# Memory's cross attention from one float32 product to three products of rounded parts

## The reference, cut to what matters

```
def memory_cross_attention(q, mem_n, w_mem_kv):
    mk, mv = jnp.split(mem_n @ w_mem_kv, 2, axis=-1)
    qh = q.reshape(B, S, XATTN_HEADS, HEAD_DIM_2)
    kh = mk.reshape(B, M, XATTN_HEADS, HEAD_DIM_2)
    vh = mv.reshape(B, M, XATTN_HEADS, HEAD_DIM_2)
    lg = jnp.einsum('bshd,bmhd->bhsm', qh, kh).astype(jnp.float32) * (HEAD_DIM_2 ** -0.5)
    p = jax.nn.softmax(lg, axis=-1).astype(q.dtype)
    return jnp.einsum('bhsm,bmhd->bshd', p, vh).reshape(B, S, C_WIDTH)
...
        out_c = memory_cross_attention(qc, mem_n, w_mem_kv[layer]) * jax.nn.silu(gc)
        y = (jax.nn.sigmoid(ma) * (out_a @ w_branch_a[layer])
             + jax.nn.sigmoid(mb) * (out_b @ w_branch_b[layer])
             + jax.nn.sigmoid(mc) * (out_c @ w_branch_c[layer]))
```

## Time and profile before

| | us |
|---|---|
| median of 3 runs | 913.99 |
| lowest and highest | 913.52, 914.01 |
| the profiled execution's own time | 914.61 |
| its span in the trace | 912.4 |
| TensorE busy in the span | 904.5 (99%) |
| VectorE busy | 610.7 (67%) |
| ScalarE busy | 507.8 (56%) |

### The profile page before, as it was taken

One profiled execution on the slowest core, in us unless ns is written; L12 is line 12 of the kernel. 1 busy time (PEld: TensorE's weight loads), 2 busy tenths in 40 slices (PEclk: granted clock), 3 DMA queues, 4 the chain that ended last, 5 costly groups with the idle time before them and its releaser, 6 DMA issues.

```text
span 912.4 us, 12831 instructions
## 1 busy us (share of the span) xinstructions
PE 904.5 (99%) x4764; PEld 764.8 (84%) x4764; DVE 610.7 (67%) x1007; ACT 507.8 (56%) x820; POOL 40.4 (4%) x53
## 2 busy tenths in 40 slices
PE   9999999999999999999999999999999999999997
PEld 7888788888888898878888888887888888888886
DVE  4897697766663756769766666386656577574665
ACT  5786655555562456665555555255557664655444
POOL 0100000440000001000000000001000000000000
PEclk9999999999999999999999999999999999999999
DMA  9844526777573577552855556354664465555651
GB/s 322 294 164 139 185 93 231 233 228 249 192 238 112 108 225 231 159 187 93 293 183 190 198 190 241 122 171 149 198 201 131 159 202 166 167 157 186 198 169 72
DMA packets 72604, 169.32 MB, mean 186 GB/s; under 512 B 11288, under 2 KB 32944, under 8 KB 71904
## 3 DMA queue, kind: packets, MB, share of 16 engines
q1 hardware_dynamic: 70080, 157.73, 53.3%
q0 software_dynamic: 2320, 10.58, 3.5%
q10 hardware_dynamic: 144, 0.20, 0.1%
HBM read 167.43 MB, written 1.06 MB: 185 GB/s over the span
## 4 chain that ended last, share of the span: by engine, by line
PE 95%; DVE 2%; DMA 1%; ACT 1%; SPq 0%; issue 0%; DVEq 0%; ACTq 0%
PE psum L851 20%; PE psum L1037 14%; PE psum L732 8%; PE psum L737 8%; PE psum L734 8%; PE psum L1040 8%; PE psum L1069 7%; PE psum L1073 4%; PE psum L962 3%; PE psum L972 3%; PE psum L966 3%; PE psum L1173 2%; PE psum L709 1%; PE psum L1208 1%; PE psum L1189 1%; DMA stage<-in_w_ab_in 1%
## 5 line engine op out<-in xcount | busy, mean ns | idle before, releaser
L1792 DVE TENSOR_TENSOR base_lo<-stage,base_hi 128x1024 fp32r<-128x1024 f32 (+3 forms) x221 | 261.1, 1206 | 103.9 <-ACT base_hi L1373 102.7
L1373 ACT CAST base_hi<-stage 128x1024 fp32r<-128x1024 f32 (+3 forms) x221 | 222.5, 1035 | 57.2 <-PE psum L737 22.5
L1792 DVE TENSOR_TENSOR extra_lo<-stage,extra_hi 128x1024 fp32r<-128x1024 f32 (+1 forms) x68 | 80.7, 1212 | 45.6 <-ACT extra_hi L1373 45.4
L732 PE MATMUL psum<-base_hi,xt 128*128 128x512 f32 (+2 forms) x256 | 100.7, 393 | 0.0
L737 PE MATMUL psum<-base_hi,xt 128*128 128x512 f32 (+2 forms) x256 | 98.4, 384 | 0.0
L734 PE MATMUL psum<-base_lo,xt 128*128 128x512 f32 (+2 forms) x256 | 98.2, 384 | 0.0
L1373 ACT CAST extra_hi<-stage 128x1024 fp32r<-128x1024 f32 (+1 forms) x68 | 68.1, 1029 | 46.8 <-PE psum L851 35.5
L851 PE MATMUL psum<-base_hi,ht 128*128 128x512 f32 x288 | 87.5, 393 | 0.3 <-DVE qk_t L2249 0.3
L1037 PE MATMUL psum<-xt,extra_hi 128*128 128x512 f32 x320 | 80.0, 392 | 0.0
L1037 PEld LDWEIGHTS psum<-xt,extra_hi 128*128 128x128 f32 x320 | 58.2, 189 | 10.8
L851 PEld LDWEIGHTS psum<-base_hi,ht 128*128 128x128 f32 x288 | 53.7, 188 | 12.5 <-DVE qk_t L2249 0.7
(11 more groups left out here) (265 smaller groups left out, 1538.9 us busy)
## 6 DMA issues: line engine op xcount, KB each, us to landing
stage<-in_w_up SPq DMA_DIRECT2D x80, 512.0 KB, 4.6
stage<-in_w_down SPq DMA_DIRECT2D x44, 512.0 KB, 4.4
stage<-in_w_in_a SPq DMA_DIRECT2D x22, 512.0 KB, 4.7
stage<-in_w_cd_in SPq DMA_DIRECT2D x16, 512.0 KB, 4.8
stage<-in_w_in_b SPq DMA_DIRECT2D x12, 512.0 KB, 3.6
stage<-in_w_ab_in SPq DMA_DIRECT2D x12, 480.0 KB, 6.8
ln_par<-in_ln POOLq DMA_DIRECT2D x4, 1024.0 KB, 7.6
stage<-in_w_ab_out SPq DMA_DIRECT2D x8, 512.0 KB, 3.7
```

What stands on the lines that cost most here:

```text
L732: pe.matmul(acc, ah, wh, start=(k == 0), stop=False)
L1373: act.copy(w_hi(c, 0, w), stage_of(c, w)).then_inc(hi_done, 1)
L1792: dve.tensor_tensor(w_lo(c, 0, w), stage_of(c, w), w_hi(c, 0, w).bitcast(F32), ALU.subtract).then_inc(lo_done, 1)
```

## The change

The cross attention gets operands in two rounded parts. ScalarE makes the high parts of keys, values and queries in the chunks 3, 4 and 5 of `gate_a`, and VectorE the low parts in the chunks 4, 5 and 6. Logits and PV are then three float32r products each: high x high, high x low, low x high. The turned probabilities are rounded by the copy that ScalarE does anyway, now to `cross_p_hi`, and VectorE subtracts this from PSUM into `cross_p_lo`: `probs_low`, the last thing in its slot s, for head s - 2. PV waits for it, and so does the next turning, since the low part is read from the bank that the turning writes.

```
@@ TensorE, slot
+                    if hd.full:
+                        pe.wait_ge(cross_p_los, h - MOBA_H + 1)
+                    for kt in range(TT) if hd.full else ():
...
+                        pe.matmul(psum[:, O_BANK, 0:S], v_hi, p_hi, start=(kt == 0), stop=False)
+                        pe.matmul(psum[:, O_BANK, 0:S], v_hi, p_lo, start=False, stop=False)
+                        last = pe.matmul(psum[:, O_BANK, 0:S], v_lo, p_hi, start=False, stop=(kt == 1))
...
                     pe.wait_ge(head_scaled, h + 1)
                     if h >= 1:
                         pe.wait_ge(p_copied, h)
+                    if h > MOBA_H:
+                        pe.wait_ge(cross_p_los, h - MOBA_H)
...
+                    if stream == "xa":
+                        n = h - MOBA_H
+                        pe.wait_ge(cross_los, 3)
+                        for t in range(TT):
...
+                            pe.matmul(acc, q_hi, cross_k_hi[:, n, :], start=True, stop=False)
+                            pe.matmul(acc, q_hi, cross_k_lo[:, n, :], start=False, stop=False)
+                            last = pe.matmul(acc, q_lo, cross_k_hi[:, n, :], start=False, stop=True)
+                        last.then_inc(logits_ready, 1)
+                        return
@@ ScalarE
-                    act.copy(probs_t[:, h % 2, 0:w], psum[:, PT_BANK, 0:w]).then_inc(p_copied, 1)
+                    turned_to = cross_p_hi if hd.full else probs_t
+                    act.copy(turned_to[:, h % 2, 0:w], psum[:, PT_BANK, 0:w]).then_inc(p_copied, 1)
...
+            def cross_hi(dst, src, made):
+                act.wait_ge(*made)
+                act.copy(dst, src).then_inc(cross_his, 1)
...
+                                  3: lambda: cross_hi(cross_k_hi[:, :, :], mem_k, read("mem_k", 2)),
+                                  4: lambda: cross_hi(cross_v_hi[:, :, :], mem_v, read("mem_v", 1)),
+                                  5: lambda: cross_hi(cross_q_hi[:, :, :], q_c, read("in_c", 2)), 7: xa_first})
@@ VectorE, slot
+                def probs_low():
+                    g = lo_h + s - 2
+                    if stream == "xa" and lo_h <= g < hi_h:
+                        dve.wait_ge(p_copied, g + 1)
+                        dve.tensor_tensor(cross_p_lo[:, g % 2, :], psum[:, PT_BANK, :],
+                                          cross_p_hi[:, g % 2, :].bitcast(F32), ALU.subtract).then_inc(cross_p_los, 1)
+
                 h = lo_h + s - 1
                 if not lo_h <= h < hi_h:
+                    probs_low()
                     return
...
                 last.then_inc(head_scaled, 1)
+                probs_low()
@@ VectorE, gate_a
+            def cross_low(count, dst, src, high):
+                dve.wait_ge(cross_his, count)
+                dve.tensor_tensor(dst, src, high.bitcast(F32), ALU.subtract).then_inc(cross_los, 1)
...
+                                  4: lambda: cross_low(1, cross_k_lo[:, :, :], mem_k, cross_k_hi[:, :, :]),
+                                  5: lambda: cross_low(2, cross_v_lo[:, :, :], mem_v, cross_v_hi[:, :, :]),
+                                  6: lambda: cross_low(3, cross_q_lo[:, :, :], q_c, cross_q_hi[:, :, :]), 7: slots("xa", 1)})
```

More of the change, by code:

```diff
@@ L305, in build_program @@
         arena = sb("arena", [P, ARENA])
+        rounded = lambda name, at, shape: nc.alloc_sbuf_tensor_at(name, [P, *shape], F32R, offset=at)
+        cross_q_hi, cross_k_hi = [rounded(f"cross_{m}_hi", arena_at + 4 * (B2 + n * XA_H * S), [XA_H, S])
+                                  for n, m in enumerate("qk")]
+        cross_v_hi = rounded("cross_v_hi", arena_at + 4 * (B2 + 2 * XA_H * S), [TT, CW])
+        cross_p_lo = rounded("cross_p_lo", arena_at + 4 * (B2 + 3 * XA_H * S), [2, 2 * S])
+        cross_q_lo = rounded("cross_q_lo", arena_at + 4 * A2, [XA_H, S])
+        cross_k_lo = rounded("cross_k_lo", arena_at + 4 * MEM_K, [XA_H, S])
+        cross_v_lo = rounded("cross_v_lo", arena_at + 4 * MEM_V, [TT, CW])
         extra_hi = nc.alloc_sbuf_tensor_at("extra_hi", [P, NS, SLOT], F32R, offset=arena_at + 4 * EXTRA)
@@ L314, in build_program @@
         pair_st = sb("pair_st", [P, 2, 5, 4])
+        probs_t_at = nc.sbuf_base
         probs_t = sb("probs_t", [P, 2, 512])
+        cross_p_hi = rounded("cross_p_hi", probs_t_at, [2, 2 * S])
         ln_par = sb("ln_par", [P, 2, D])
@@ L362, in build_program @@
         p_turned, p_copied = sem("p_turned"), sem("p_copied")
+        cross_his, cross_los, cross_p_los = sem("cross_his"), sem("cross_los"), sem("cross_p_los")
         pv_ready, head_done = sem("pv_ready"), sem("head_done")
@@ L1094, in slot @@
                         pe.wait_ge(head_done, h)
-                    for kt in range(TT):
-                        first = 0 if hd.full else kt * P
+                    if hd.full:
+                        pe.wait_ge(cross_p_los, h - MOBA_H + 1)
+                    for kt in range(TT) if hd.full else ():
+                        cut = (slice(None), kt, slice((h - MOBA_H) * HD2, (h - MOBA_H + 1) * HD2))
+                        v_hi, v_lo = cross_v_hi[cut], cross_v_lo[cut]
+                        p_hi, p_lo = [m[:, h % 2, kt * S:(kt + 1) * S] for m in (cross_p_hi, cross_p_lo)]
+                        pe.matmul(psum[:, O_BANK, 0:S], v_hi, p_hi, start=(kt == 0), stop=False)
+                        pe.matmul(psum[:, O_BANK, 0:S], v_hi, p_lo, start=False, stop=False)
+                        last = pe.matmul(psum[:, O_BANK, 0:S], v_lo, p_hi, start=False, stop=(kt == 1))
+                    for kt in () if hd.full else range(TT):
+                        first = kt * P
                         last = pe.matmul(psum[:, O_BANK, first:S], hd.v(kt),
@@ L1115, in slot @@
                     hd = head_of(2 * PAIRS + h)
[L1116 to L1120, removed]
                     if h >= 1:
@@ L1123, in slot @@
                     n0 = keys0(hd)
+                    if stream == "xa":
+                        n = h - MOBA_H
+                        pe.wait_ge(cross_los, 3)
+                        for t in range(TT):
+                            acc = psum[:, LOGIT_BANK, t * S:(t + 1) * S]
+                            q_hi, q_lo = [m[:, n, t * P:(t + 1) * P] for m in (cross_q_hi, cross_q_lo)]
+                            pe.matmul(acc, q_hi, cross_k_hi[:, n, :], start=True, stop=False)
[3 more added lines that the diff above has]
+                        return
+                    pe.wait_ge(qk_copied, h + 1)
+                    q, k = qk_t[:, h % 2, 0:S], qk_t[:, h % 2, S:2 * S]
                     for t in range(TT):
@@ L1730, in xa_first @@
                 slot("xa", 1)
+            def cross_hi(dst, src, made):
+                act.wait_ge(*made)
+                act.copy(dst, src).then_inc(cross_his, 1)
             act.wait_ge(x_ready, 16)
             gemm("gate_a", gate, {0: lambda: make_gates("in_c", 3, 5), 1: lambda: turn("b", ht_hi, 6, [0]),
-                                  2: lambda: turn("b", ht_hi, 6, [1]), 7: xa_first})
+                                  2: lambda: turn("b", ht_hi, 6, [1]),
+                                  3: lambda: cross_hi(cross_k_hi[:, :, :], mem_k, read("mem_k", 2)),
+                                  4: lambda: cross_hi(cross_v_hi[:, :, :], mem_v, read("mem_v", 1)),
+                                  5: lambda: cross_hi(cross_q_hi[:, :, :], q_c, read("in_c", 2)), 7: xa_first})
             gemm("branch_a", None, {s: slots("xa", s + 1) for s in range(1, 6)})
@@ L2327, in _ @@
                                 7: lambda: [scale_gates("in_c", 3), gate_b([5])]})
+            def cross_low(count, dst, src, high):
+                dve.wait_ge(cross_his, count)
+                dve.tensor_tensor(dst, src, high.bitcast(F32), ALU.subtract).then_inc(cross_los, 1)
             gemm("gate_a", None, {1: lambda: turn("b", ht_hi, ht_lo, 6, [0]), 2: lambda: turn("b", ht_hi, ht_lo, 6, [1]),
-                                  7: slots("xa", 1)})
+                                  4: lambda: cross_low(1, cross_k_lo[:, :, :], mem_k, cross_k_hi[:, :, :]),
+                                  5: lambda: cross_low(2, cross_v_lo[:, :, :], mem_v, cross_v_hi[:, :, :]),
+                                  6: lambda: cross_low(3, cross_q_lo[:, :, :], q_c, cross_q_hi[:, :, :]), 7: slots("xa", 1)})
             def branch(n):
```

## The result

The changed kernel takes 917.11 us (median of 6 runs, 916.52 to 917.83), the kernel before 913.91 in the same comparison. The ratio is 1.0036 with a 95% interval of 1.0023 to 1.0049: slower by 3.2 us. Forecast was 916.9. The profiled execution of the changed kernel took 917.83 us, its span is 915.6.

The account below looks back on a forecast made before the run. The prediction took TensorE's queue to bound the kernel. Three waits lost 4.05 us, products saved 1.16 and `gate_a` cost 0: +2.9 us, taking the median from 913.99 to 916.9 us, range 915.2 to 918.1.

Parts of the forecast that it names:

- Where the bound lies: Attention slots: time is the length of TensorE's queue, busy 99% of the span; a new wait there would add time.
- The products: Logits and PV: six float32r products at 0.119 us replace 0.86 us; eight groups save 1.16 us.
- `gate_a` at nothing: Three casts and three subtractions in `gate_a` cost 0; the query's low part has 0.14 us of cover.
- The wait: PV of heads 0, 1 and 2 each waits 4.11 - 2.76 = 1.35 us for the probabilities' low part.
- The terms on VectorE: From logits' end to low part's end: 0.04 + 2.31 + 0.74 + 0.69 = 3.78 us.
- Release and cold pipe: PV's restart after VectorE's low part: 0.06 + 0.11, plus 0.16 in the chain's time, 0.33 us in all.
- No cancelling: Across the slots the three waits don't cancel; the period between PV becomes 5.99 us against 4.92.
- No wait for head 3: PV of head 3: low part comes at most 2.5 us and two releases behind PV 2's start, wanted at 3.93.
- The sum: Whole kernel: 4.05 lost, 1.16 saved, 0 for `gate_a`, so +2.9 us, median 916.9 us.
- One stall only: Rival for PV's waits: TensorE pays 1.35 us once, VectorE then runs ahead; 914.2 us, chance 0.08.
- no wait at all: Rival for PV: the wait is hidden and only the products' saving counts; 912.8 us, chance 0.05.
- The two others: Rivals: `gate_a` too full, +0.4, 917.3 us, chance 0.15; PV's stalls smaller, 915.9 us, chance 0.12.

Follow-up runs that it names:

- the wait alone: Against the kernel before: float32 attention, nothing rounded, only VectorE's unused subtraction last in each slot and PV waiting for it; 918.06 us, ratio 1.0041.
- another order of VectorE: Changed kernel with low part behind the negated maxima, chunk's split behind the scaling, evacuations of `branch_a`'s first half behind slot 5; 912.82 us, ratio 0.9987.
- the parts alone: Changed kernel keeping `gate_a`'s casts and subtractions and the first logits' wait for them, but all attention products float32; 913.87 us, ratio 0.9997.
- the doubled subtraction: Changed kernel with each subtraction of the turned probabilities done twice, first into a buffer nobody reads; 918.77 us, ratio 1.0049.
- the single late low part: Against the kernel at 912.82 us: in slot 2 alone the low part stands last, as in the change; 914.32 us, ratio 1.0002.
- the first logits with the doubled subtraction: Against the kernel at 912.82 us: the subtraction for the queries' low part in `gate_a` done twice; 914.01 us, ratio 0.9999.
- the order with the evacuations left in place: Against the kernel at 912.82 us: evacuations stay ahead of slot 3, split still behind the scaling; 914.01 us, ratio 0.9999.

## Why the prediction was right, point by point

- **Where the bound lies.** TensorE's queue, and the new wait in it: shown by the wait alone (918.06 us) and by its absence in another order of VectorE (912.82).
- **The products.** Forecast 0.119 us each, by L1073; they show 0.12, and six take 0.72. The saving of 1.16 us stands in the logits' 0.16 a group (forecast 0.145) and in the 1.0 us by which the other order's chain beats that of the kernel before, with one wait of 0.2 us left in it. The prediction leaves out that the Trainium skill, page "TensorE: Matmul & The Clock Gate", section "Back-to-back issue gap", gives its formula for an isolated product, without the weight loads; the estimate from it is 109 ns, and the trace with a weight load beside each product shows 0.12 us.
- **`gate_a` at nothing.** Right, at 913.87 us with the parts alone. The cover was 0.23 us, forecast 0.14 and 0.06 of release.
- **The wait.** Forecast 1.35 us three times. From the logits' end (794.28 + 0.13 = 794.41) to the turn of PV's first product (798.32 + 0.36 - 0.12 = 798.56) are 4.15 us, less a chunk of 2.76: 1.39. The terms on VectorE were met within 0.02 each. Release and cold pipe were 0.15 + 0.24 = 0.39 instead of 0.33: this is the one term that was short, by 0.06 a wait. The release alone was 0.15 where 0.06 was forecast, and the restart 0.24 where 0.27 was; that the sum came nearer than its parts is luck.
- **No cancelling.** Period 6.02, forecast 5.99. That the loop is closed is shown by the doubled subtraction (each of three waits grew by 0.6) and by the single late low part, which no later slot made good.
- **No wait for head 3.** Right: its first product shows 0.12 us.
- **The sum.** 3 x 1.39 - 1.16 = 3.0 us; forecast 2.9. The chain shows it: from the second turning in `gate_a` to the end of PV 3 are 39.45 us before and 42.47 after. The medians differ by 3.2. The rest of 0.2 lies ahead of that turning in the two profiles (772.56 and 772.76 us) and was not followed up; it is within the scatter of the runs.
- **The rivals.** One stall only, and no wait at all, did not come; the reason given against them (the maxima start right behind the logits) is what the runs showed. The second of them names the right remedy by the wrong gap: 0.69 us doesn't fit in VectorE's idle 0.21, but with the chunk's split moved out of the way the whole time up to the reciprocal is free. Even with the split left there, no PV waited: the reciprocal came 0.3 us later and only the turnings paid (913.42 us). The two others did not come either: `gate_a` kept its cover, and the stalls were larger than forecast, not smaller.

## What to carry to other kernels

On an engine with a third of its time idle, the place of a small instruction can matter more than its length: a subtraction of 0.68 us at the end of three slots cost 4 us, and in the order at 912.82 us, where it fills a time in which the same engine waits for another, nothing. Before a subtraction or copy is put on a helper engine, follow the loop from the bound engine's output back to its next input, and compare the loop with the bound engine's own work in one round; here the excess was paid in every round. And look at what the freed place collides with next: with a chunk's split behind the scaling and two evacuations of 1.2 us in all behind that, 1.1 us were lost again, as much as the cheaper products had saved.

## What the runs showed of the hardware that was not expected

A product that waits for VectorE starts later than one case of before suggests. At 395 us it began 0.06 us behind the end of VectorE's instruction. PV's first product in the changed kernel began 0.15 behind it (798.17 to 798.32), in the kernel with the wait alone 0.14, and the first logits with the doubled subtraction 0.14; in the order with the evacuations left in place PV's was 0.15. In the kernel with the low part early and the split ahead of the reciprocal, the turning that waited for the scaling had its weight load 0.06 behind the end of this instruction (797.53 to 797.59); VectorE in order of time:

```profile
796.91 0.62 DVE L1956 TENSOR_SCALAR pair_probs<-pair_probs,soft 128x256 f32<-128x256 f32 x2
```

And the weight load of PV's first product in the changed kernel:

```profile
798.28 0.19 PEld L1112 LDWEIGHTS psum<-cross_p_hi,cross_v_hi 128*128 128x128 f32 x1 [1.57 <-issue]
```

What makes the difference was not tried. The waits that took longer stand last in the list of waits of their instruction in the code, and the trace ascribes the weight load's idle time to issue, where the turning's is ascribed to VectorE; more than that the runs don't tell. The first product behind a wait then shows 0.36 us where the next ones show 0.12.
